# A hybrid decoder layer on one core: the last token tile added and routed by halves, its norm rows on ScalarE and GpSimd, four ring loads held until the gathers landed

## The reference

```
hn   = rms_norm(x);  q, k, v, b, c, u = split(hn @ w_in)
attn = diff_attention(q, k, v) (4 heads);  conv = rms_norm(b * conv3(c * u))
h    = x + concat(attn, conv) @ w_out
hn2  = rms_norm(h) * ffn_norm_gain
group = argmax of 4 group logits; top 2 of that group's 8 expert logits (hn2 @ routers)
out  = h + sum over the two experts of weight * (silu(hn2 @ w_gate[e]) * (hn2 @ w_up[e])) @ w_down[e]
```

## Time and profile before

| what | value |
|---|---|
| median of 3 runs | 1171.34 us (1168.75 to 1176.4) |
| the profiled execution | 1170.99 us |
| its span, first to last instruction | 1169.2 us |
| mean granted TensorE clock | 0.981 |
| busy | PE 1100.5 us (94%), DVE 850.7 (73%), ACT 678.5 (58%), POOL 355.1 (30%) |
| DMA | 253.64 MB, mean 217 GB/s |
| busiest group of DVE | L2015 wlo, 190 x 2286 ns |

### The profile page before, as it was taken

One profiled execution on the slowest core, in us unless ns is written; L12 is line 12 of the kernel. 1 busy time (PEld: TensorE's weight loads), 2 busy tenths in 40 slices (PEclk: granted clock), 3 DMA queues, 4 the chain that ended last, 5 costly groups with the idle time before them and its releaser, 6 DMA issues.

```text
span 1169.2 us, 15426 instructions
## 1 busy us (share of the span) xinstructions
PE 1100.5 (94%) x5629; PEld 864.2 (74%) x5629; DVE 850.7 (73%) x1210; ACT 678.5 (58%) x1001; POOL 355.1 (30%) x431
## 2 busy tenths in 40 slices
PE   5999999999879998888889999999999999999995
PEld 4999999889658787777667777777777777766663
DVE  6635364445676776767668999889889889888893
ACT  6424232322465555443367877877877877777783
POOL 2333333234321111111104334344344344322220
PEclk9999999999999999999699999999999999999998
DMA  8021030302402112331979999999999999999972
GB/s 243 2 70 39 18 91 1 108 18 73 130 2 91 43 67 91 126 131 68 344 274 359 371 375 379 375 369 373 376 376 376 369 374 362 369 356 361 373 309 44
DMA packets 77403, 253.64 MB, mean 217 GB/s; under 512 B 18832, under 2 KB 43408, under 8 KB 52752
## 3 DMA queue, kind: packets, MB, share of 16 engines
q1 hardware_dynamic: 70160, 235.85, 54.3%
q0 software_dynamic: 7168, 16.79, 6.1%
HBM read 240.03 MB, written 20.97 MB: 223 GB/s over the span
## 4 chain that ended last, share of the span: by engine, by line
PE 43%; DMA 7%; DVE 3%; ACT 1%; issue 1%; POOL 0%; POOLq 0%; DVEq 0%; ACTq 0%
PE banks L2094 9%; PE banks L2096 9%; PE banks L2095 9%; DMA raw<-in_w_gate 6%; PE banks L2113 4%; PE banks L2111 4%; PE banks L2115 4%; PE banks L2070 2%; DVE wlo L2015 1%; DMA rows<-xn_rows,table_i 1%; PE banks L2079 1%; ACT whi L1964 1%; DMA out<-y_sb,table_i 0%; DVE hn L1206 0%; PE banks L1637 0%
## 5 line engine op out<-in xcount | busy, mean ns | idle before, releaser
L2015 DVE TENSOR_TENSOR wlo<-raw,whi 128x2048 fp32r<-128x2048 f32 x190 | 427.6, 2286 | 50.4 <-ACT whi L1964 50.2
L1964 ACT CAST whi<-raw 128x2048 fp32r<-128x2048 f32 x188 | 353.7, 1910 | 31.0 <-DMA raw<-in_w_gate 18.6
L1946 POOL DMA_INDIRECT out<-y_sb,table_i x32 | 154.0, 4811 | 198.9 <-ACT y_sb L1982 193.7
L2094 PE MATMUL banks<-whi,rT_hi 128*96 128x512 f32 x512 | 207.3, 405 | 6.0 <-DVE wlo L2015 5.4
L2096 PE MATMUL banks<-whi,rT_lo 128*96 128x512 f32 x512 | 203.6, 398 | 0.0
L2095 PE MATMUL banks<-wlo,rT_hi 128*96 128x512 f32 x512 | 202.4, 395 | 0.0
L2094 PEld LDWEIGHTS banks<-whi,rT_hi 128*96 128x96 f32 x512 | 83.3, 163 | 41.2 <-DVE wlo L2015 6.0
L2096 PEld LDWEIGHTS banks<-whi,rT_lo 128*96 128x96 f32 x512 | 83.1, 162 | 36.5
L2095 PEld LDWEIGHTS banks<-wlo,rT_hi 128*96 128x96 f32 x512 | 83.7, 163 | 31.6
L1937 POOL DMA_INDIRECT rows<-xn_rows,table_i x30 | 48.3, 1610 | 188.9 <-PE banks L2070 181.4
L862 ACT ACTIVATE qk_sq<-banks 128x256 f32<-128x256 f32 x32 | 12.3, 385 | 128.6 <-PE banks L1495 128.6
(11 more groups left out here) (248 smaller groups left out, 2067.6 us busy)
## 6 DMA issues: line engine op xcount, KB each, us to landing
raw<-in_w_gate SPq DMA_DIRECT2D x64, 1024.0 KB, 23.1
raw<-in_w_up SPq DMA_DIRECT2D x64, 1024.0 KB, 23.5
raw<-in_w_down SPq DMA_DIRECT2D x64, 1024.0 KB, 24.5
c_raw<-in_w_in SPq DMA_DIRECT2D x12, 512.0 KB, 3.8
q_raw<-in_w_in SPq DMA_DIRECT2D x12, 512.0 KB, 6.4
x_stage<-in_x SPq DMA_DIRECT2D x8, 512.0 KB, 6.5
wo_raw<-in_w_out SPq DMA_DIRECT2D x2, 2048.0 KB, 8.0
h_sb<-in_x SPq DMA_DIRECT2D x8, 512.0 KB, 4.8
```

The lines of the kernel that those rows point to most:

```text
L1946: pool.indirect_dma_start(out=s.out_rows, out_offset=bass.IndirectOffsetOnAxis(ap=s.table_i[:, e:e + 1], axis=0), in_=s.y_sb[e % 2][:], in ...
L1964: act.copy(s.w_hi[i % HI][:], s.raw[i % RING][:]).then_inc(s.hi_ready, 1)
L2015: dve.tensor_tensor(s.w_lo[i % RING][:], s.raw[i % RING][:], s.w_hi[i % HI][:].bitcast(F32), ALU.subtract).then_inc(s.lo_ready, 1)
L2094: pe.matmul(o, s.rT_hi[e % 2][:, c, :], hi[:, c4, :], start=(c == 0), stop=False)
```

## The change

- **w_out's buffers.** The conv half (n = 1) now lies whole, hi and lo, at 8 to 40 KB, the attention half at 40 to 72 KB. The transposed x is split by token half in the same places. The instructions that use them are the same in number and shape.
- **SP.** Ring tiles 7 to 10 are loaded when the last tile's second conv product is done (`half_done` 4*NT-2), ahead of the last h store. Tiles 11 to 14 are loaded after both first gathers have landed (`rows_in`).
- **DVE.** `add_x(NT-1, 0)` comes ahead of tile 6's `choose_group`, `add_x(NT-1, 1)` right after it. `normalise_h(NT-1)` is gone; DVE waits for `hn_ready` before `table_i`.
- **ACT.** `square_last_h(0)` ahead of tile 6's `exponent_gates`; `exponent_top(NT-2)` behind `copy_hnT(NT-1, 1)`; new `scale_last_h`: two activations, h times its norm factor, into `hn`.
- **POOL.** Two multiplies of 128 x 512, `hn` times the gain, in place.
- **PE.** The last tile's routing product in two halves of four chunks, each behind its transposes; `count_tile(NT-2)` behind both. WARM is 16.

```diff
+    CONV_KEYS = (7, 11)
-    WARM = 24
+    WARM = 16
@@ SP
+                if i == NT - 1:
+                    sp.wait_ge(half_done, 4 * NT - 2)
+                    for j in range(CONV_KEYS[0], CONV_KEYS[1]):
+                        s.load_tile(sp, j)
                 sp.wait_ge(h_ready, 2 * i + 2)
                 sp.dma_start(s.out_rows[t * P:(t + 1) * P, :], s.h_sb[b][:]).then_inc(h_stored[b], 16)
-                if i == NT - 1:
-                    sp.wait_ge(half_done, 4 * NT)
-                    s.load_tile(sp, sum(len(row) for row in EARLY))
...
-            for i in range(sum(len(row) for row in EARLY) + 1, RING):
+            for e in range(2):
+                sp.wait_ge(s.rows_in[e], 16)
+            for i in range(CONV_KEYS[1], RING):
                 s.load_tile(sp, i)
@@ POOL
             rstd_h(NT - 1)
+            for n in range(2):
+                q = slice(n * P // 2, (n + 1) * P // 2)
+                hn = s.hn[:].rearrange("p c q -> p q c")[:, q, :]
+                pool.wait_ge(last_scaled, n + 1)
+                pool.wait_ge(gain2_in, 16)
+                pool.tensor_tensor(hn, hn, s.gain2[:].rearrange("p (q c) -> p q c", c=KC)[:, q, :], ALU.mult).then_inc(hn_ready, 1)
@@ ACT
+            def scale_last_h():
+                act.wait_ge(h_rstd_ready, NT)
+                act.wait_ge(h_squared, NT + 1)
+                for n in range(2):
+                    q = slice(n * P // 2, (n + 1) * P // 2)
+                    act.activation(s.hn[:].rearrange("p c q -> p q c")[:, q, :],
+                                   s.h_sb[(NT - 1) % 2][:].rearrange("p (q c) -> p q c", c=KC)[:, q, :], ACT.Identity,
+                                   scale=s.h_rstd[:, (NT - 1) % 2:(NT - 1) % 2 + 1]).then_inc(last_scaled, 1)
...
             copy_logits(NT - 2)
+            square_last_h(0)
             exponent_gates(NT - 2)
-            exponent_top(NT - 2)
-            square_last_h(0)
             copy_hnT(NT - 1, 0)
             square_last_h(1)
             copy_hnT(NT - 1, 1)
+            exponent_top(NT - 2)
+            scale_last_h()
             copy_logits(NT - 1)
@@ DVE
             finish_parts()
+            add_x(NT - 1, 0)
             choose_group(NT - 2)
+            add_x(NT - 1, 1)
             choose_first(NT - 2)
             choose_second(NT - 2)
-            add_x(NT - 1, 0)
             weigh_tokens(NT - 2)
             fill_entries(NT - 2, NT - 1)
-            add_x(NT - 1, 1)
             place_tile(NT - 2)
             finish_parts()
-            normalise_h(NT - 1)
...
             dve.wait_ge(s.table_summed, 1)
+            dve.wait_ge(hn_ready, 2 * NT)
@@ PE
-            def route_tile(i, g):
+            def route_tile(i, g, parts=(0, 1)):
...
-                pe.wait_ge(hnT_copied, 2 * i + 2)
+                pe.wait_ge(hnT_copied, 2 * i + parts[-1] + 1)
...
-                for c in range(KC):
+                for c in [4 * part + c for part in parts for c in range(4)]:
...
             turn_h(NT - 1, 0)
+            route_tile(NT - 1, None, (0,))
+            turn_h(NT - 1, 1)
+            route_tile(NT - 1, None, (1,))
             count_tile(NT - 2)
-            turn_h(NT - 1, 1)
-            route_tile(NT - 1, None)
```

More of the change, by code:

```diff
@@ L168, in layer_kernel @@
         lamd = at("lamd", 6.375, [P, 4])
-        xT_hi = at("xT_hi", 8, [P, 2, KC, T // 2], F32R)
-        xT_lo = at("xT_lo", 40, [P, 2, KC, T // 2], F32R)
+        xT_hi = [at(f"xT_hi{h}", 8 + 32 * h, [P, KC, T // 2], F32R) for h in range(2)]
+        xT_lo = [at(f"xT_lo{h}", 24 + 32 * h, [P, KC, T // 2], F32R) for h in range(2)]
         kvq = at("kvq", 72, [P, NT, 2048])
@@ L198, in layer_kernel @@
         k_tm = [at(f"k_tm{b}", (205, 5)[b], [P, 2, 2, DK]) for b in range(2)]
-        wo_hi = at("wo_hi", 8, [P, KC, D], F32R)
-        wo_lo = at("wo_lo", 40, [P, KC, D], F32R)
-        wo_raw = at("wo_raw", 40, [P, KC, D])
+        wo_hi = [at(f"wo_hi{n}", 40 - 32 * n, [P, CT, D], F32R) for n in range(2)]
+        wo_lo = [at(f"wo_lo{n}", 56 - 32 * n, [P, CT, D], F32R) for n in range(2)]
+        wo_raw = [at(f"wo_raw{n}", 56 - 32 * n, [P, CT, D]) for n in range(2)]
         probs = [at(f"probs{b}", 152 + 4 * b, [P, T]) for b in range(2)]
@@ L433, in front @@
     h_rstd_ready = sem("h_rstd_ready")
+    last_scaled = sem("last_scaled")
     hn_ready = sem("hn_ready")
@@ L514, in tile_of, with wo_at @@
     def tile_of(xT, t):
-        return xT[:, t // 4, :, t % 4 * P:(t % 4 + 1) * P]
-    def wo_at(k):
-        return (k + CT) % KC
+        return xT[t // 4][:, :, t % 4 * P:(t % 4 + 1) * P]
+    def wo_at(w, k):
+        return w[k // CT][:, k % CT, :]
     def score_cols(m, n):
@@ L962, in round_wo_conv @@
                 act.wait_ge(taps_in, 16 * (CT + 1))
-                act.activation(s.wo_hi[:, m, :], s.wo_raw[:, m, :], ACT.Identity, scale=s.conv_taps[:, m, 3:4]).then_inc(wo_hi_ready, 1)
+                act.activation(s.wo_hi[1][:, m, :], s.wo_raw[1][:, m, :], ACT.Identity, scale=s.conv_taps[:, m, 3:4]).then_inc(wo_hi_ready, 1)
             def split_hi(i):
@@ L1037, in _ @@
                     act.wait_ge(wo_in[0], 16)
-                    act.copy(s.wo_hi[:, wo_at(k), :], s.wo_raw[:, wo_at(k), :]).then_inc(wo_hi_ready, 1)
+                    act.copy(wo_at(s.wo_hi, k), wo_at(s.wo_raw, k)).then_inc(wo_hi_ready, 1)
                 if conv_of(g) is not None:
@@ L1310, in low_wo_conv @@
                 dve.wait_ge(wo_hi_ready, m + 1)
-                dve.scalar_tensor_tensor(s.wo_lo[:, m, :], s.wo_raw[:, m, :], s.conv_taps[:, m, 3:4],
-                                         s.wo_hi[:, m, :].bitcast(F32), ALU.mult, ALU.subtract).then_inc(wo_lo_ready, 1)
+                dve.scalar_tensor_tensor(s.wo_lo[1][:, m, :], s.wo_raw[1][:, m, :], s.conv_taps[:, m, 3:4],
+                                         s.wo_hi[1][:, m, :].bitcast(F32), ALU.mult, ALU.subtract).then_inc(wo_lo_ready, 1)
             def split_lo(i):
@@ L1421, in _ @@
                     dve.wait_ge(wo_hi_ready, CT + k + 1)
-                    dve.tensor_tensor(s.wo_lo[:, wo_at(k), :], s.wo_raw[:, wo_at(k), :], s.wo_hi[:, wo_at(k), :].bitcast(F32),
+                    dve.tensor_tensor(wo_at(s.wo_lo, k), wo_at(s.wo_raw, k), wo_at(s.wo_hi, k).bitcast(F32),
                                       ALU.subtract).then_inc(wo_lo_ready, 1)
@@ L1507, in multiply_unit @@
                     pe.wait_ge(c_lo_ready, KC * j + c + 1)
-                    pe.matmul(o, w_hi[:, c, :], s.xT_hi[:, half, c, :], start=(c == 0), stop=False)
-                    pe.matmul(o, w_hi[:, c, :], s.xT_lo[:, half, c, :], start=False, stop=False)
-                    ins = pe.matmul(o, w_lo[:, c, :], s.xT_hi[:, half, c, :], start=False, stop=(c == KC - 1))
+                    pe.matmul(o, w_hi[:, c, :], s.xT_hi[half][:, c, :], start=(c == 0), stop=False)
+                    pe.matmul(o, w_hi[:, c, :], s.xT_lo[half][:, c, :], start=False, stop=False)
+                    ins = pe.matmul(o, w_lo[:, c, :], s.xT_hi[half][:, c, :], start=False, stop=(c == KC - 1))
                 if 1 in parts:
@@ L1633, in multiply_out @@
                         pe.wait_ge(oT_ready, HEADS * i + k + 1)
-                    kk = wo_at(k + CT if q < 2 else k)
+                    kk = k + CT if q < 2 else k
                     hi = s.mc_hi[:, k, :] if q < 2 else s.ma_hi[i % 2][:, k, :]
                     lo = s.mc_lo[:, k, :] if q < 2 else s.ma_lo[i % 2][:, k, :]
-                    pe.matmul(o, hi, s.wo_hi[:, kk, cols], start=(q < 2 and k == 0), stop=False)
-                    pe.matmul(o, hi, s.wo_lo[:, kk, cols], start=False, stop=False)
-                    ins = pe.matmul(o, lo, s.wo_hi[:, kk, cols], start=False, stop=(q >= 2 and k == 3))
+                    pe.matmul(o, hi, wo_at(s.wo_hi, kk)[:, cols], start=(q < 2 and k == 0), stop=False)
+                    pe.matmul(o, hi, wo_at(s.wo_lo, kk)[:, cols], start=False, stop=False)
+                    ins = pe.matmul(o, lo, wo_at(s.wo_hi, kk)[:, cols], start=False, stop=(q >= 2 and k == 3))
                 ins.then_inc(half_done, 1)
@@ L1665, in route_tile @@
                     pe.wait_ge(mapsA_copied, SLOTS_2)
-                for c in range(KC):
+                for c in [4 * part + c for part in parts for c in range(4)]:
                     ins = pe.matmul(ps[:, 4, 128:128 + GROUPS + E], s.hnT[:, c, :], s.w_route[:, c, :], start=(c == 0), stop=(c == KC - 1))
-                ins.then_inc(routed, 1)
+                if 1 in parts:
+                    ins.then_inc(routed, 1)
             def count_first():
```

4 lines of the change are left out of this document (1 added, 3 removed).

## The result

| | before | changed |
|---|---|---|
| median of 7 runs each | 1171.34 us (1168.75 to 1176.4) | 1162.87 us (1159.02 to 1166.6) |
| ratio, 95% interval | | 0.9922 [0.9904, 0.994] |
| profiled execution / its span | 1170.99 / 1169.2 us | 1164.27 / 1162.5 us |
| mean granted clock | 0.981 | 0.989 |

The changed kernel is 8.5 us faster (0.8%), which lies within the 1% that the chances call the same. It was run once more beside the last experiments: 1164.48 us against 1171.15, ratio 0.9948 [0.9931, 0.9965]. So the two measurements put the gain at 6 to 9 us.

What follows compares the result with a forecast made beforehand. The prediction took the expert stage as bound by two streams of nearly one speed, PE and the DMA engines. Gains of 3.4 + 4.4 + 2.0 = 9.8 us took 1171.34 to 1161.5 us, range 1159 to 1168.

Steps and rivals of the forecast that it cites:

- Step A: Last tile's routing in the drain: the new order brings `table_i` 3.4 us sooner (2.0 to 4.2).
- Step B: From `table_i` to first transposes: gather without other loads, 5.9 us instead of 10.3, gain 4.4 (3.4 to 4.7).
- Step C: First expert tile: TensorE's clock stays up for the first 12 matmuls, gain 2.0 us (0 to 2.4).
- Step D: Expert stage: four loads held until after the gathers fit into idle DMA time, cost 0, at worst 5.6 us.
- the third rival: Drain: GpSimd's multiplies and DVE hold each other up, giving 1165.3 or 1163.2 us; chance 0.12.
- Two signs that I had named: Expert stage: ACT's waits for raw not longer in all; forecast wrong if the gain of 580 us has shrunk by 1100.
- (1): First expert tile: the clock falls all the same, gain 7.8 us, time 1163.5; chance 0.22.
- (2): First gather: its time is its own and not the loads', so only 3.4 us gained, 1167.9; chance 0.10.
- (4): Expert stage: the stream pays for the held loads in full, 9.8 - 5.6 us gained, 1167.1; chance 0.06.
- the one mechanism that could make it slower: Drain: GpSimd's multiplies, some 7 us each, land `hn` so late that all gains go; chance 0.03, over 1% slower.

Runs made afterwards that it cites:

- e9: The changed kernel itself, run and profiled a second time beside the last experiments: 1164.48 us, 0.9948 of the kernel before.
- e1: Changed kernel with DVE, ACT, POOL and PE in the order of before, new loads and WARM = 16 kept: 1164.01 us, 0.9936.
- e4: Changed kernel with the last tile's norm rows made by DVE again, no scaling on ACT, no multiplies on POOL: 1163.76 us, 0.9927.
- e5: Changed kernel with each of GpSimd's two multiplies cut into four of 128 x 128: 1164.2 us, 0.995.
- e6: Changed kernel with GpSimd's multiplies started only after DVE has finished tile 6's placing: 1163.89 us, 0.9946.
- e10: Changed kernel with all eight ring tiles 7 to 14 loaded after the gathers: 1173.46 us, 1.0015.
- e11: Changed kernel with 8 warm-up matmuls instead of 16: 1164.35 us, 0.9946.
- e2: Changed kernel with the ring loads and WARM = 24 of before, only the drain's order and engines changed: 1168.92 us, 0.9977.
- e3: Changed kernel with ring tiles 11 to 14 loaded right behind the last norm rows, not after the gathers: 1168.53 us, 0.9973.
- e7: Changed kernel with 24 warm-up matmuls instead of 16: 1166.68 us, 0.9956.
- e8: Changed kernel with tiles 11 and 12 loaded right behind the last norm rows, only 13 and 14 held: 1161.8 us, 0.9931.
- e12: Changed kernel with GpSimd's multiplies in eight pieces, tiles 11 and 12 loaded behind the norm rows, WARM = 12: 1164.46 us, 0.9938.

## Why the prediction was right, point by point

The time was 1162.87 us for 1161.5 forecast, inside 1159 to 1168. The steps are less good than the sum: A gave 1.1 us less than forecast, B and C 1.3 more, and D took 1 to 2. That they nearly cancel is luck.

**Step A** was mis-sized: 3.4 us forecast, 2.26 measured (+16.59 to +14.33; 2.1 in e9). The term that failed is DVE's way to tile 7's choice, with nothing in it for GpSimd: the third rival came true beside the forecast, and DVE was held 2.05 us. Without the hold the choice would have begun at +5.8, 4.3 us sooner than before and 0.9 sooner than forecast (+6.7), since in this execution the clock stayed at 2.4 GHz through both halves of the routing product (2 x 1.05 us, where I had taken 1.8 for the second) and PE was done at +4.4, not +5.3. In e9 there was no such help: the second half took 1.89 us, PE was done at +5.3 as forecast, DVE was held 1.36 us (1.81 for the pair instead of 0.45), and without that the choice would have begun at +6.6. In both, the multiplies ended at +7.6 and set the choice. I had taken the multiplies as free cover; the rival had put the DVE side at up to 2.6 us less 0.9 of spare, which was the right place and nearly the right price. I gave it 0.12 as an alternative, when it was compatible with the rest and should have been a term of the sum.

Also too cheap in step A: ACT's scalings took 2.12 us for two, not 1.3. They write every 512 bytes, and I took the price of a dense copy; that the stride is the reason is likely, but no run parts it from the rest. GpSimd's took 1.5 each, within what I gave. The norm rows landed at 566.29, 1.9 us ahead of the gather, as forecast, though the store itself took 5.43 us: I had the engines empty from about 558 us on, but they were full until about 564 (share 1.02 from 556 to 560, 0.98 from 560 to 564), and the last h store, issued at 554.31 behind the four loads, took 10.7 us. The rows landed at +13.0 all the same, where the forecast had +11.9 to +13.4; of the 1.9 us of cover 1.1 came from the later table.

**Step B** was right in kind and a little small: 4.4 forecast, 5.22 measured, above my upper bound of 4.7. The gather landed after 4.49 us, below the 5.9 that I had as nearest row, and the 16 matmuls ended after 5.04. My floor of 5.6 for them came from the kernel before; over the runs with 16 they took 4.96 to 6.49 us with the moment at which the clock rises, and in e1, e4, e5, e6 and e10 the transposes waited for them, not for the gather.

**Step C** was right: 2.3 us for the twelve matmuls (2.0 forecast), 0.2 more between transposes and first matmul. e11 shows that it hangs on the warm-up.

**Step D** was forecast at 0 and cost about 1 us (1.5 and 2.0 in the two profiled executions). The account was right, that the work held back must fit into the idle share: for e10 it gave 8 us, and 8.1 were paid. But it left a margin of only 0.5 us (8.1 - 5.6 - 2.0), and which of the three terms was off is not shown. Two signs that I had named went against me here: ACT's waits for gate and up weights from 590 us on grew from 26.3 to 34.9 us, and by expert 31's mark, 1085 us, the lead had shrunk from 10.0 to 8.5.

The sum at the first expert tile was 9.98 us for 9.8 forecast; at expert 31 it was 8.5.

**The rivals.** (1), the clock falls: not by the first expert tile, in any kernel with 12 or more warm-up matmuls and a quick gather. (2), the gather has its own time: refuted by e2 and e3. (3) came true in part. (4), the stream pays in full: a fifth to a third of its 5.6 us, but it is a real mechanism, and e10 shows the kernel that ends on the other side by it, 1.0015. I had named GpSimd as the one mechanism that could make it slower; holding too many loads was the nearer one. What remains open is the exact price of four held loads, and why the first run of the changed kernel gained 8.5 us and the second 6.7; their intervals overlap only from 0.9931 to 0.9940, and neither ratio lies in the other's.

## What to carry to other kernels

When two engines' streams run at nearly one speed, a transfer on the critical path is cheapest when the queue is emptied for it, and the price is that the work held back must find idle time later: count that idle time first, and hold back no more than it. Work moved off a busy VectorE to GpSimd isn't free if GpSimd works on SBUF at the same moment: here VectorE waited for the same 2 us that it had been spared. A warm-up in front of a wait wants to last as long as the wait: much shorter, and the clock falls again before the work comes (e11); longer, and the work waits for it (e7).

## What the runs showed of the hardware

- A gather of 96 rows of 4 KB took 4.2 to 4.5 us from its issue with the DMA engines free, 4.3 (e8) and 5.1 (e12) beside the end of two loads, 9.7 to 10.5 with four to eight loads of 1 MB issued ahead of it. Four held it up as long as eight did.
- A GpSimd multiply of 128 x 512 holds a tiny instruction of VectorE (128 x 4) until it has ended: 1.37 and 1.55 us instead of 0.23 and 0.21. A reduction (0.22 us) and an instruction with one input in PSUM (0.22 us) weren't held.
- ScalarE writing every 512 bytes took 1.06 us for 128 x 512 (two scalings in 2.12), where a dense write of the same size took 0.63 (the squares); the two instructions differ in more than that.
- The same 16 matmuls took 4.96 to 6.49 us from one kernel to the next, since TensorE's clock rose from 1.2 to 2.4 GHz at another moment of them: in e9 (4.97 us) the granted clock was 1.00 from 568 us on, 2.8 us behind their start; in e5 (6.49 us) it was still 0.50 at 569, 5.3 us behind it.
